# The even mixer of a transformer trunk laid out as one stream of projections, with its small steps at written places

## The reference, cut to what matters

```python
def gla_ssd_mixer(h, w_in, ...):
    q, k, v, g, a_low, z, xbc, dt = jnp.split(h @ w_in, points, axis=-1)
    q = q.reshape(b_, t, GLA_HEADS, GLA_DK) * (GLA_DK ** -0.5)          # 4 heads, 128 wide
    log_a = jax.nn.log_sigmoid((a_low @ gla_w_gate2 + gla_b_gate2)) / GLA_GATE_NORMALIZER
    o = gla_chunked(q, k, v, log_a)                                     # v: 4 heads, 256 wide
    o = rmsnorm(o, gla_norm_w) * jax.nn.silu(g)
    xbc = jax.nn.silu(causal_depthwise_conv(xbc, conv_w, conv_b))       # 4 taps
    xs, bm, cm = jnp.split(xbc, ...)                                    # 16 heads of 64, 4 groups
    dt = jax.nn.softplus(dt + dt_bias); a = -jnp.exp(a_log)
    y = ssd_chunked(xs * dt[..., None], dt * a, bm, cm) + d_skip * xs
    y = rmsnorm((y * jax.nn.silu(z)).reshape(b_, t, 4, 256), ssm_norm_w)
    return jnp.concatenate([o_gla, y], axis=-1) @ w_out
```

## Time and profile before

| | us |
|---|---|
| median of 3 runs | 2367.57 |
| lowest, highest | 2367.52, 2368.17 |
| profiled execution, its time | 2367.07 |
| profiled execution, its span | 2365.3 |

### The profile page before, as it was taken

One profiled execution on the slowest core, in us unless ns is written; L12 is line 12 of the kernel. 1 busy time (PEld: TensorE's weight loads), 2 busy tenths in 40 slices (PEclk: granted clock), 3 DMA queues, 4 the chain that ended last, 5 costly groups with the idle time before them and its releaser, 6 DMA issues.

```text
span 2365.3 us, 25040 instructions
## 1 busy us (share of the span) xinstructions
PE 2239.2 (95%) x10358; PEld 1812.3 (77%) x10358; DVE 1009.8 (43%) x1438; ACT 739.3 (31%) x1141; POOL 193.0 (8%) x128
## 2 busy tenths in 40 slices
PE   7999999798888888999999999999998789999999
PEld 6888888677765666888888888888886348888887
DVE  4333224458876665443332343332265335333322
ACT  4222223433333333332221232222233434322211
POOL 0000001332212120000000000000033000000000
PEclk9999999899998889999999999999999779999999
DMA  5332332221111112242323232323222002332331
GB/s 180 95 102 89 107 98 71 79 71 45 54 36 37 43 36 101 69 134 89 107 89 107 72 125 92 104 89 107 90 83 75 15 0 71 118 106 89 107 98 54
DMA packets 55298, 197.31 MB, mean 83 GB/s; under 512 B 6272, under 2 KB 6784, under 8 KB 55184
## 3 DMA queue, kind: packets, MB, share of 16 engines
q1 hardware_dynamic: 53856, 193.75, 25.4%
q10 hardware_dynamic: 1328, 1.96, 0.2%
HBM read 193.58 MB, written 2.10 MB: 83 GB/s over the span
## 4 chain that ended last, share of the span: by engine, by line
PE 61%; DVE 4%; issue 3%; ACT 2%; POOL 1%; DVEq 0%; ACTq 0%; POOLq 0%
PE ps L789 11%; PE ps L790 11%; PE ps L791 11%; PE ps L797 7%; PE ps L799 7%; PE ps L798 7%; PE ps L1162 1%; PE ps L1161 1%; DVE a_rows L1226 1%; ACT a_rows L415 1%; ACT a_rows L727 1%; DVE a_rows L1223 1%; DVE temps L1223 1%; PE ps L1042 0%; PE ps L1172 0%
## 5 line engine op out<-in xcount | busy, mean ns | idle before, releaser
L789 PE MATMUL ps<-h_hi,w_hi 128*128 128x512 f32 (+1 forms) x1976 | 746.8, 378 | 12.4 <-DVE temps L1599 9.2
L791 PE MATMUL ps<-h_hi,w_lo 128*128 128x512 f32 (+1 forms) x1976 | 734.4, 372 | 0.0
L790 PE MATMUL ps<-h_lo,w_hi 128*128 128x512 f32 (+1 forms) x1976 | 733.9, 371 | 0.0
L415 ACT ACTIVATE w_hi<-raw 128x1024 fp32r<-128x1024 f32 x352 | 370.5, 1056 | 790.5 <-PE ps L799 392.4
L1223 DVE TENSOR_TENSOR w_lo<-raw,w_hi 128x1024 fp32r<-128x1024 f32 x288 | 343.7, 1221 | 338.0 <-ACT w_hi L415 337.4
L789 PEld LDWEIGHTS ps<-h_hi,w_hi 128*128 128x128 f32 x1976 | 376.4, 190 | 86.1 <-issue 21.1
L791 PEld LDWEIGHTS ps<-h_hi,w_lo 128*128 128x128 f32 x1976 | 376.2, 190 | 64.3
L790 PEld LDWEIGHTS ps<-h_lo,w_hi 128*128 128x128 f32 x1976 | 376.6, 191 | 61.8 <-issue 2.5
L1223 DVE TENSOR_TENSOR a_rows<-a_rows,ps 128x512 f32<-128x512 f32 x88 | 60.5, 688 | 614.0 <-PE ps L791 614.0
L797 PE MATMUL ps<-w_hi,a_hi 128*128 128x512 f32 x704 | 274.4, 390 | 0.0
L799 PE MATMUL ps<-w_hi,a_lo 128*128 128x512 f32 x704 | 274.0, 389 | 0.0
(11 more groups left out here) (182 smaller groups left out, 1918.9 us busy)
## 6 DMA issues: line engine op xcount, KB each, us to landing
raw<-in_w_gate_up SPq DMA_DIRECT2D x176, 512.0 KB, 3.7
raw<-in_w_down SPq DMA_DIRECT2D x88, 512.0 KB, 3.5
raw<-in_w_xbc SPq DMA_DIRECT2D x16, 512.0 KB, 3.5
raw<-in_w_zg SPq DMA_DIRECT2D x16, 512.0 KB, 3.5
raw<-in_w_even_out SPq DMA_DIRECT2D x16, 512.0 KB, 3.6
raw<-in_w_qk_small SPq DMA_DIRECT2D x9, 512.0 KB, 3.5
raw<-in_w_v SPq DMA_DIRECT2D x8, 512.0 KB, 3.5
raw<-in_w_odd_out SPq DMA_DIRECT2D x8, 512.0 KB, 3.5
```

Of the source, the lines that this page charges most:

```text
L415: return nc.scalar.activation(to, source, ACT.Copy, scale=scale)
L789: nc.tensor.matmul(to, w_h, hi, start=first, stop=False)
L790: nc.tensor.matmul(to, w_h, lo, start=False, stop=False)
L791: return nc.tensor.matmul(to, w_l, hi, start=False, stop=last)
```

## The change

The mixer's projections become one stream with 520 places, a place being one triple of matmuls. A generator (`projections`) yields after each triple; `project_to(place)` runs the stream up to a place. `plan_even` gives each small step of PE its place, and ACT and DVE go by the same places: `keep_up(place)` first takes, convolves and splits what the stream has finished up to there.

- Weights: `vg` (16 slots: v for two heads, g for two, v, g) in token layout, then `xbc0`, `z01`, `xbc12`, `z2`, `xbc3`, `z3`, by group; z in token layout, z2 and z3 in blocks of 256 columns.
- Four PSUM banks (0 to 3) serve the stream, four (4 to 7) the small steps. v, g and z tiles are taken by ACT (copy or silu) straight from PSUM, q and k too. A conv tile is started by ACT from PSUM, and DVE adds three taps, reading PSUM. 4 of the 16 conv tiles fall into the heads, 12 into the groups.
- Heads and groups give their outputs with tokens on the partitions. The norm's sums are made by ACT (square with accumulation) and the factor is a column, so the column sums and the spread on PE go; eight transposes for each head and group turn the gated rows back, and ACT and DVE split them from PSUM at once into the rows of the concatenation (`cat_high`, `cat_low`). The concatenation's rows are ready as the stream reaches the output weights, whose first half begins at place 320.
- The decay of an SSM head is now one product over 32 partitions, `source_rows` by `head_rows`, which gives differences of the cumulated decays directly; the exponential of a spread row falls away, and the far part is scaled by a column. The skip term is a product with a diagonal.
- The log decays are made one head ahead inside the heads; exp and ln of the logits are one instruction each over all four heads. The step sizes are computed in head 0.
- POOL makes low parts until the last head ends (slot 25 of the stream), DVE from there on. The two gain loads of the mixer move to slot 11 of `even_out` and wait for the last turned group.

```diff
+AHEAD = 7
...
+def plan_even():
+    at = {}
+    for h in range(GH):
+        base = 12 + 41 * h
+        for j, step in enumerate((0, 3, 7, 10, 14, 17, 22)):
+            at["level", h, j] = base + step
+        at["own", h], at["far", h], at["out", h], at["head_turn", h] = base + 25, base + 30, base + 36, base + 65
+    for g in range(SG):
+        base = 12 + 41 * GH + 45 * g
+        for name, step in (("x", 0), ("cb", 13), ("skip", 18), ("group_turn", 52)):
+            at[name, g] = base + step
+        for r in range(4):
+            at["decay", g, r] = base + (4, 9, 17, 22)[r]
+            at["near", g, r] = base + (19, 22, 27, 31)[r]
+    tile_end = [128 + 8 * (n + 1) + (32 if n >= 4 else 0) + (16 if n >= 12 else 0) for n in range(16)]
...
@@ gpsimd @@
+                    for norm in range(GH):
+                        while n < min(stream + (even_at["out", norm] + 4) // 8 + 4, GROUPS_LOW):
+                            split_low(n)
+                            n += 1
+                        power(norm)
+                    for norm in range(GH, GH + SG):
+                        power(norm)
...
@@ scalar @@
+                def split_to(place):
+                    while upcoming["slot"] < min(stream + place // 8 + 4, INNER_END):
+                        split_high(upcoming["slot"])
+                        upcoming["slot"] += 1
...
+                    for j in range(len(SPANS)):
+                        keep_up(even_at["level", h, j] - AHEAD)
+                        decay_of(j)
...
+                def take_z(place):
+                    while upcoming["z"] < 3 and (192, 272, 320)[upcoming["z"]] <= place:
...
+                def group(g):
...
+                    silu_x(g)
+                    head_row(0)
+                    head_row(1)
+                    keep_up(even_at["x", g] + 4)
+                    exponential(0)
+                    head_row(2)
+                    clear(even_at["x", g] + 7)
+                    turn_group(g - 1) if g else turn_head(GH - 1)
+                    conv_to(tile_end[4 * g + 3])
+                    silu_bc(g)
+                    exponential(1)
...
+                    act.wait_ge(y_gated, g + 1)
...
+                    act.wait_ge(rstd_col_ready, norms[("ssm", g)] + 1)
+                    for c in range(NC):
+                        copy(token_rows[c], token_rows[c], rstd_col[:, c:c + 1]).then_inc(y_scaled, 1)
+                split_to(-40)
+                take(1)
+                take(2)
+                take(3)
+                take(4)
+                split_to(-32)
+                take(5)
+                split_to(-24)
+                act.wait_ge(dt_signal, 1)
+                nc.scalar.activation(far1, far1, ACT.Exp, scale=-1.0)
+                nc.scalar.activation(a_log, a_log, ACT.Exp).then_inc(dt_act, 1)
+                act.wait_ge(logit_ready, GH)
+                after(nc.scalar.activation(temps[:, 0:GH, :], temps[:, 0:GH, :], ACT.Exp, scale=-1.0))
+                nc.scalar.activation(a_rows[:, 34:34 + GH, :], temps[:, 0:GH, :], ACT.Ln, bias=1.0).then_inc(softplus_ready, 1)
...
@@ tensor @@
+                def projections():
...
+                    for n in range(4):
+                        pe.wait_ge(z_taken, 4 + n + 1)
+                        yield from tile(stream + 34 + n, n)
...
+                def project_to(place):
+                    while placed[0] < place:
+                        next(projecting)
+                        placed[0] += 1
...
+                    for j in range(len(SPANS)):
+                        project_to(even_at["level", h, j])
+                        pe.wait_ge(gla_factors, h * 8 + (j + 1))
...
@@ vector @@
+                def conv_to(place):
+                    while upcoming["tile"] < 16 and tile_end[upcoming["tile"]] <= place:
...
+                            stt(row[:, back:T], ps[:, n % 4, 0:T - back], conv_w[:, of, 3 - back:4 - back], row[:, back:T],
+                                ALU.mult, ALU.add).then_inc(conv_step if back < 3 else conv_done, 1)
...
+                    for j in range(len(SPANS) + 1):
+                        if j < len(SPANS):
+                            keep_up(even_at["level", h, j] - AHEAD)
                             differences(j)
-                        if j == 3:
-                            tap(0, 1)
+                        if j == 1 and h:
+                            head_mean(h - 1)
                         if j:
                             factors(j - 1)
...
+                        if j >= 2:
+                            merge(j - 2)
+                        if j == 2 and h + 1 < GH:
+                            log_decay(h + 1)
+                        if j == 3 and h == 0:
+                            step_sizes()
```

More of the change, by code:

```diff
@@ new lines, in even @@
+                nc.scalar.activation(exp_cum, cum_early, ACT.Exp)
+                act.wait_ge(dt_cum, 2)
+                nc.scalar.activation(far1[:, 0:3 * P], far1[:, 0:3 * P], ACT.Exp).then_inc(dt_act, 1)
+                for h in range(1, GH):
+                    head(h)
+                for g in range(SG):
+                    group(g)
+                turn_group(SG - 1)
+                act.wait_ge(group_squares, 4 * SG)
+                out_stage(EVEN, upcoming["slot"], (even_at["group_turn", SG - 1] - 320) // 8)
@@ new lines, in group @@
+                    last.then_inc(y_far_done, 1)
+                first_four(s)
+                project_to(-32)
+                pe.wait_ge(even_in, 48)
+                pe.wait_ge(small_taken, 1)
+                pe.wait_ge(tile_taken, QK0 + 3)
+                for h in range(GH):
+                    last = nc.tensor.matmul(ps[:, 4 + h, :], gate2[:, h * P:h * P + P], rows(a_rows, SMALL)[A_LOW:A_LOW + RANK, :], start=True, stop=True)
+                last.then_inc(decay_logits, 1)
+                for h in range(GH):
+                    head(h)
@@ L1680, in ssm_groups @@
-                    after(last)
-                    take(3)
-                    for m in range(2):
-                        dve.wait_ge(row_silu, g * 4 + (m + 3))
-                        row = rows(a_rows, g + (Q + GH * m))
-                        last = tt(row, row, scaled[m], ALU.mult)
-                    last.then_inc(group_done, 1)
+                    keep_up(even_at["near", g, 3] + 7)
+                    pair = token_pair.rearrange("p (c v) -> p c v", c=2)
+                    dve.wait_ge(y_far_done, g + 1)
```

1191 lines of the change are left out of this document (648 added, 543 removed).

## The result

The changed kernel takes 2353.04 us (median of 4; 2349.92 to 2354.97) against 2367.87 us (2367.52 to 2368.54) before it: a ratio of 0.9936, 95% interval 0.9919 to 0.9953. It is faster, by 0.6%. The forecast was 2300 us with a range of 2268 to 2342, so the time lies outside it: 15 us gained where 67 were forecast.

What follows compares the result with a forecast made beforehand. TensorE, busy 95% of the span, was taken to lose time only by idling (72 us) and low clock in the even mixer. 2367 - 101 removed + 34 of returning waits = 2300 us, range 2268 to 2342.

Steps and rivals of the forecast that it cites:

- both rivals near it: Whole kernel: places hide nearly everything, 2273 us (chance 0.10); or half of today's waits per small step stay, 2321 us (0.25).
- points 3 to 5: Even mixer's small steps: heads -4 us, groups +2 us, 256-column z matmuls +1.3 us, changes between stream and small step +1.5 us.
- Point 6: Waits that come back in the even mixer's start, heads, groups and output: 24 us of idling, 34 us with its clock.
- level 3 of head 0: Even mixer's heads: PE waits 5 us (2 to 9) while DVE does head 1's log decay and the dt chain.
- The tile after z2: Group 2: the place 6 after x waits about 4 us, as ACT silus z2 only after exp(0) and the next head row.
- the DMAs priced at zero: Mixer's gain loads on SP's queue and ACT's three constant loads cost nothing; without cover each would cost one weight load.
- Point 2: Even mixer: of 91.6 us at 1.2 GHz, removing the low clock gains 30 us, between 9.8 and 45.8.
- 0.42: Even mixer: price in us of low clock for each us of PE idling.
- 1.42: Factor on returning idle time, counting its low clock too: 24 us of idling cost 34 us.
- ring dry: Weight stream: PE meets an unsplit slot at each of 43 slots, 147 us back, 2413 us; chance 0.06.
- no gain: Even mixer's small steps: each waits the full 0.92 us, 110 us back, 2376 us; chance 0.04.
- half the gain: Even mixer's small steps: half of today's 0.92 us wait stays at each, 55 us back, 2321 us; chance 0.25.

Runs made afterwards that it cites:

- the layout mended: Changed kernel with mixer_cols 200 columns wide and not 172, moving the buffers behind it up by 96 bytes: 2305.11 us, ratio 0.9739 to the kernel before.
- The three runs that follow it: On the 200-column layout: ScalarE and VectorE reordered, 2275.93 us; with that, the start's low parts by VectorE, 2279.64; or all the mixer's low parts by VectorE, 2274.10.
- The seven profiled layouts of the kernel before: Kernel before unmoved; buffers behind mixer_cols moved 32, 64 or 128 bytes; a alone 32; all buffers 32; h 64 and a 192: 2363.85 to 2404.51 us.
- the three of the changed kernel with its waits: Changed kernel as it is, 2353.04 us; with the buffers behind mixer_cols 32 bytes further, 2332.21 us; 96 bytes further, 2305.11 us.
- the shorter lead: Heads' level steps 3 places ahead of their products and not 7 (AHEAD), against the reordered changed kernel with 200-column mixer_cols: 2318.41 us, 42 us more.
- the three waits: Changed kernel with 200-column mixer_cols, reordered: head rows before gated rows, z2 two places earlier, gating before next convolution and low parts: 2275.93 us, ratio 0.9612.

## Why the prediction was wrong, point by point

**The step that failed** is the first sentence on the windows: "The change touches only the even mixer". From it came "A place costs 0.68 us" as a constant, and FFNs left out of the sum. The diff showed the wider `mixer_cols`, and I read it as 40 more columns of data. It moved h and a against the weights by 160 bytes, and that costs 41.5 us in the four FFNs and, by the sum below, some 6 in the even mixer and 1 in the odd one. Undone by 96 unused bytes, the changed kernel runs in 2305.11 us, 48 us less and 5 us from the forecast. The range, and both rivals near it, were ranges of the mixer alone.

**The mixer.** It was forecast 67 us shorter and is 59.7 shorter (stage table). Idle time fell by 41.8 us, the loss to the clock by 19.6; 1.7 us of it came back by the slower steps and points 3 to 5 together. The kernel with the layout mended has the steps of the kernel before and parts the two: there the mixer is 58.7 us shorter, idle time 40.3 and clock 14.0, which leaves -4.4 us for points 3 to 5, forecast at +0.8, and with it about +6 for the steps. (The three runs that follow it leave -3 to -4 as well.) So the bound was read rightly: idling and low clock were what the change took away. The 7.3 us that the mixer fell short are 6 of slower steps and 6 of waits, less 5 of small steps that came cheaper than forecast.

**Point 6, waits that come back**: forecast 24 us, found 30.
- Start 2.5 forecast, 2.95 found; level 3 of head 0 5 forecast, 2.55 found, since four scans took 1.37 us unblocked and not the 2.7 taken from the blocked row; heads 1 to 3 6 forecast, 5.5 found in seven waits.
- Groups 10 forecast, 18.9 found. The tile after z2 was named at 4 and is 2.85. What I had not seen are the 7.3 us of the differences behind the head rows: I went through ScalarE's order for z, B and C and stopped at the scaled rows, without asking what is queued behind them.
- Output 0 to 2 forecast, 0.1 found; the DMAs priced at zero cost nothing that shows.

**Point 2, the clock.** Removed 30, come back 10: 20 us were forecast and 19.6 measured. That is in part luck. The seven profiled layouts of the kernel before idle 69 to 72 us in this mixer and lose 31 to 44 to the clock; the three of the changed kernel with its waits idle 30 to 33 and lose 12 to 24. From the means (38.4 and 18.1 us, idle time 70.5 and 31.8) comes a price of 0.52 us for each us of idling, and 0.51 with the shorter lead. So 0.42 was low by little, if at all, and one pair of executions doesn't measure it.

**The upper end.** The upper ends of point 6 add up to 50 us, which at 1.42 gives 2367 - 101 + 71 = 2337 us and not 2342; the measured time lies beyond either.

**The table loads.** The Trainium skill ("ScalarE: Activation LUTs", What ACT_TABLE_LOAD costs) would have put a drain behind each and 16 us on the sum. In the changed kernel a load of 1.28 us at 773.57 is followed by its function at 774.86, and half of its 31 loads have their function within 0.012 us of their end; no drain is seen, and leaving it out of the sum was right.

**The marks set beforehand.** Idle 20 to 30 us: 30. Clock of the groups 0.95: 0.95. A head 44 to 46 us: from level 0 to level 0 they take 49.3, 49.2 and 43.7, the long ones with the waits of head 0 and the dt columns. A group 49 to 51: 49.8 for the first, 59.2 and 62.1 for the next two, with their waits at either clock. The mixer 544 us: 550.4, and 551.5 with the layout mended, where the clock took 5.6 us more. Largest waits at level 3 of head 0 and after z2: 2.55 and 2.85, level with the 2.95 at the start and the head rows' 2.6 and 3.1. Conv taps not stretched by GpSimd: the four that ran beside a low part took 0.75 us, like the others. **Rivals**: ring dry is excluded, since no wait for a low part stands among TensorE's in the mixer of the changed kernel; no gain is too, with 30 us of idling and not the 77 it needed; half the gain (2321) needed waits at most levels, and six of 28 waited. The measured 2353 us lies between the last two, and for a reason that neither names.

## What to carry to other kernels

A change of a buffer's size is a change of every address behind it: before forecasting, compare the distances between the operands of the matmuls that carry the time, and, for products like these, keep moving and stationary operands a multiple of 256 bytes apart. When stages that the edit does not touch change length, look at the step of one instruction there before looking at the edit. For a stream with small steps in it, go down each helper engine's queue and ask of every operation whether it depends on the wait ahead of it; here such reordering took 12 to 14 us of idling out of the mixer. And before a clock gain is booked to an edit, compare it with other executions that idle as much.

## What the runs showed of the hardware

- At the full clock a 512-column matmul in float32 halves steps 226.7 ns when the moving and the stationary operand's partition addresses differ by a multiple of 256 bytes, 228.9 at 64, and 232.4 to 234.3 at 32, 96, 128, 160, 192 and 224. With every buffer 32 bytes higher the step stayed at 226.7 ns. In this kernel the distance is worth 2% of the whole (2353.04 and 2305.11 us). Other widths and strides were not tried. The Trainium skill ("SBUF — State Buffer", SBUF: two separate sides) says that only the pair of ports that VectorE and GpSimd share causes contention and that TensorE never waits on anyone. These runs don't show TensorE waiting on another engine, but its speed does depend on where its own two operands lie. Why, and why 64 is nearly free, was not shown.
- A low part on GpSimd stops VectorE's two-input operations for its whole length: four took 10.19 us beside 9.99 us of GpSimd. The same section of the Trainium skill calls the ports an exclusive lock, and the traces agree. Taking 30 such low parts of 2.4 us away from GpSimd freed 28 us of VectorE, most of the 37 that doing them itself costs it.
- The odd mixer, the same code in all kernels, took 263 to 275 us in the profiled executions. Windows of it with the mended layout, then with the three waits taken away:

```profile
1659.90:1931.40 271.50, 241.06 (x972) 163.53 (x971) 119.49 (x208) 99.04 (x216) 41.45 (x26) 0.87 0.16 49
```

```profile
1637.80:1900.90 263.10, 231.72 (x971) 160.28 (x970) 119.48 (x208) 98.77 (x216) 41.45 (x25) 0.92 0.16 51
```

The idle time is 30.4 and 31.4 us, the granted clock 0.87 and 0.92, and the work lost 29.0 and 18.5 us to it. So 8 to 10 us between two kernels, or two executions of one (2269.5 to 2284.7 in one case), can come from where the spells at 1.2 GHz fall; differences of 0.3% between these versions are not told apart by a few executions.
- The best version is the three waits with the mended layout, 2275.93 us, or 2274.10 with all low parts on VectorE, which the intervals do not tell apart: 0.961 of the kernel before and 0.967 of the changed one.
